# Six tiles' gates worked out in the last tile, gate matrices by ScalarE, fewer routing steps

## What is computed

```python
def hier_moe(h, w_group, b_group, w_expert, b_expert, w_gate_up, w_down):
    gl = tok @ w_group + b_group
    p_group = softmax(gl);  p_top, g_idx = top_k(p_group, 1)
    el = (tok @ w_expert + b_expert).reshape(-1, N_GROUPS, EXPERTS_PER_GROUP)
    e_val, e_idx = top_k(take_along_axis(el, g_idx), TOP_K)
    e_w = softmax(e_val) * p_top                  # the two gates of a token
    for e in range(N_EXPERTS):                    # 16 experts, D_EXPERT = 256
        gu = tok @ w_gate_up[e]
        act = silu(gu[:, :256]) * gu[:, 256:]
        y = y + gates[:, e:e + 1] * (act @ w_down[e])
```

## Time and profile before

| | us |
|---|---|
| median of 3 runs | 980.98 (979.95 to 981.66) |
| profiled execution | 977.75 |
| its span | 975.9 |
| PE busy | 927.5 (95%) |
| DVE busy | 593.3 (61%) |
| ACT, POOL busy | 234.6 (24%), 217.0 (22%) |
| mean granted TensorE clock | 0.995 |

### The profile page before, as it was taken

The page is one execution under the profiler, slowest core; times in us unless marked ns, Lnnn a source line. Parts: engine busy times, 40 slices in busy tenths (PEclk is TensorE's granted clock), DMA queues, the critical chain, the costliest instruction groups (busy, mean ns, idle before and its releaser), DMA issues.

```text
span 975.9 us, 19077 instructions
## 1 busy us (share of the span) xinstructions
PE 927.5 (95%) x7577; PEld 681.8 (70%) x7577; DVE 593.3 (61%) x1812; ACT 234.6 (24%) x606; POOL 217.0 (22%) x302
## 2 busy tenths in 40 slices
PE   5999999999999999999999998889999999999995
PEld 5787687596686868769769676565667666777663
DVE  2366775784685687487578468988534324345443
ACT  1233331431431342234143233231010111111010
POOL 7020020020011002002002000400244454465653
PEclk9999999999999999999999999999999999999998
DMA  8920101020010110110100002812557976979621
GB/s 305 395 91 1 45 22 45 1 66 22 23 66 1 45 45 22 44 36 32 44 2 23 21 24 71 339 67 66 179 171 238 343 232 215 346 260 357 219 91 57
DMA packets 51491, 113.99 MB, mean 117 GB/s; under 512 B 11191, under 2 KB 14519, under 8 KB 51392
## 3 DMA queue, kind: packets, MB, share of 16 engines
q1 hardware_dynamic: 35072, 87.07, 24.9%
q0 software_dynamic: 14592, 25.22, 7.7%
q10 hardware_dynamic: 1728, 0.31, 0.2%
HBM read 112.54 MB, written 25.17 MB: 141 GB/s over the span
## 4 chain that ended last, share of the span: by engine, by line
PE 78%; DVE 16%; DMA 2%; issue 2%; ACT 1%; SPq 0%; POOL 0%; POOLq 0%; DVEq 0%; ACTq 0%
PE pm L417 71%; PE pm L420 6%; DVE pqkv L1405 4%; DMA w_sb<-in_w_in 2%; DVE X L1558 1%; DVE bs L1623 1%; DVE sc L1628 1%; DVE xT L1344 1%; DVE hT L1360 1%; PE pm L798 1%; DMA qkvT<-h_mid,w_sb 0%; DVE V_S L1636 0%; DVE xT L1223 0%; ACT pqkv L978 0%; DVE y_mix L1649 0%
## 5 line engine op out<-in xcount | busy, mean ns | idle before, releaser
L417 PEld LDWEIGHTS pm<-hT,w_sb 128*128 128x128 f32 x1544 | 177.0, 194 | 9.5 <-DVE hT L1360 6.0
L417 PE MATMUL pm<-hT,w_sb 128*128 128x128 f32 x1544 | 178.9, 278 | 4.9 <-DVE hT L1360 4.3
L417 PE MATMUL pm<-w_sb,hT 128*128 128x512 f32 (+1 forms) x384 | 148.1, 534 | 0.4 <-DMA w_sb<-in_w_in 0.4
L1918 POOL TENSOR_TENSOR tail<-tail,rows 128x512 f32<-128x512 f32 x8 | 10.2, 1269 | 511.4 <-ACT aTm L999 511.4
L417 PE MATMUL pm<-wo_sb,pT 128*128 128x512 f32 x256 | 115.0, 596 | 2.8 <-ACT pT L1046 2.1
L417 PEld LDWEIGHTS pm<-w_sb,hT 128*128 128x128 f32 x384 | 70.7, 191 | 57.1 <-issue 52.9
L417 PE MATMUL pm<-ctmp,w_sb 128*128 128x128 f32 x768 | 88.8, 276 | 1.1 <-DVE ctmp L1706 1.1
L1405 DVE SCALAR_TENSOR_TENSOR pqkv<-ci,cw,pqkv 128x128 f32<-128x128 f32 x288 | 77.6, 344 | 19.9 <-ACT pqkv L978 19.6
L417 PEld LDWEIGHTS pm<-ctmp,w_sb 128*128 128x128 f32 x768 | 86.7, 192 | 2.6 <-issue 2.0
L417 PEld LDWEIGHTS pm<-wo_sb,pT 128*128 128x128 f32 x256 | 46.7, 190 | 53.0 <-issue 49.3
L1778 DVE TENSOR_TENSOR ci<-pm,gain 128x512 f32<-128x512 f32 x32 | 20.6, 686 | 82.6 <-PE pm L798 48.7
(11 more groups left out here) (315 smaller groups left out, 1527.0 us busy)
## 6 DMA issues: line engine op xcount, KB each, us to landing
w_sb<-in_w_gate_up SPq DMA_DIRECT2D x12, 2048.0 KB, 14.8
w_sb<-in_w_down SPq DMA_DIRECT2D x12, 1024.0 KB, 6.5
w_sb<-in_w_in SPq DMA_DIRECT2D x4, 2048.0 KB, 20.5
wo_sb<-in_w_gate_up SPq DMA_DIRECT2D x4, 2048.0 KB, 14.6
xt<-in_x SPq DMA_DIRECT2D x8, 512.0 KB, 4.4
xT<-in_x_turned SPq DMA_DIRECT2D x8, 512.0 KB, 3.5
wo_sb<-in_w_out SPq DMA_DIRECT2D x1, 4096.0 KB, 21.8
sc<-in_x SPq DMA_DIRECT2D x8, 512.0 KB, 3.5
```

What stands on the lines that cost most here:

```text
L417: return pe.matmul(o_, lhsT=l_, rhs=r_, start=start, stop=stop, skip_group_check=True)
L1918: g.tensor_tensor(qk_in[:, 0:QH, :], qk_in[:, 0:QH, :], gqk[:, None, 0:DH].broadcast_to([P, QH, DH]), ALU.mult)
```

## The change

It has four parts.

1. `rsqrt_one` replaces `rsqrt` for the two factors of one column each (the norm of x in `row_factors`, the norm before the experts in `factor`): ten steps in place of twelve, 16 times in the program.
2. `route_experts` and `route_rows` do both choices in one instruction of twice the width: 2 steps in place of 4, and 6 in place of 10.
3. The gates of the first six tiles are worked out in `late(7)` between `add_x(0)` and `add_x(1)` (five steps). They are divided by the token's number (`gate_by_row`; one more step makes the reciprocals `by_row`), and ScalarE makes `hot_gate[u]` as `hot_row[u]` times that factor. TensorE sums 12 of the 16 gate products between the counts and the half slots, where `keep_busy` products stood; the last four come behind `turn_halves(0)`, and the two halving products behind `gate_up_halves(0)`. `hot_mod` 0 to 7 lie in a new place (`more`), since `ci` is written earlier than they are last read.
4. In the routing of the last two tiles each pair of `row_hots` signals by itself (`R.hots`), the sum that needs the new picks comes last, and `rows_of` reads pm[0] directly, with the copy to `table` behind it.

```diff
+EARLY_HOTS = [c * NT + t for c in range(TOPK) for t in range(AHEAD)]
+LATE_HOTS = [c * NT + t for c in range(TOPK) for t in range(AHEAD, NT)]
...
             keep_busy(pm[3], 3)
+            pe.wait_ge(A.rank_ready, 1)
+            mm(pm[1][:, 0:n], ones[:, :], before, True, False)
             pe.wait_ge(R.picks, 1)
-            pe.wait_ge(A.rank_ready, 1)
-            mm(pm[1][:, 0:n], upper_strict, picks[:, AHEAD * NE:], True, False)
...
-            mm(pm[1][:, 0:n], ones[:, :], before, False, True).then_inc(R.counts, 1)
+            mm(pm[1][:, 0:n], upper_strict, picks[:, AHEAD * NE:], False, True).then_inc(R.counts, 1)
...
-            keep_busy(pm[3], 4)
-            pe.wait_ge(R.hots, 1)
-            for u in late_hots:
-                ins = mm(pm[0][:, 0:P], hot_mod[u], hot_row[u], False, u == late_hots[-1])
+            def add_gates(first, last):
+                for i, u in enumerate((EARLY_HOTS + LATE_HOTS)[first:last]):
+                    pe.wait_ge(R.gate_hots, first + i + 1)
+                    ins = mm(pm[5][:, 0:P], hot_mod[u], hot_gate[u], first + i == 0, u == LATE_HOTS[-1])
+                return ins
+
+            add_gates(0, 8)
+            for i, u in enumerate(LATE_HOTS):
+                pe.wait_ge(R.hots, i + 1)
+                ins = mm(pm[0][:, 0:P], hot_mod[u], hot_row[u], False, u == LATE_HOTS[-1])
             ins.then_inc(R.rows_summed, 1)
-            keep_busy(pm[3], 1)
-            pe.wait_ge(R.rows_ready, 1)
+            add_gates(8, len(EARLY_HOTS))
+            pe.wait_ge(R.rows_ready, 2)
...
-            keep_busy(pm[3], 2)
+            keep_busy(pm[3], 1)
             turn_rows(0)
...
+                if i < NE:
+                    turn_halves(i)
                 if i == 0:
                     sum_gates()
-                if i < NE:
-                    turn_halves(i)
...
                 gate_up_halves(i)
+                if i == 0:
+                    sum_half_gates()
...
+            def gate_hot(u):
+                act.activation(hot_gate[u], hot_row[u], ACT.Copy,
+                               scale=gate_by_row[:, u // NT, u % NT:u % NT + 1]).then_inc(R.gate_hots, 1)
+            act.wait_ge(A.hots, TOPK * AHEAD + 1)
+            for u in EARLY_HOTS:
+                gate_hot(u)
             act.wait_ge(R.exp_in, 1)
...
+            act.wait_ge(R.hots, len(LATE_HOTS) + 1)
+            for u in LATE_HOTS:
+                gate_hot(u)
...
+            def rsqrt_one(step, y, a, tmp, src, scale):
+                step(v.tensor_scalar(a, src, scale, EPS, ALU.mult, ALU.add))
+                step(v.tensor_scalar(y.bitcast(I32), a.bitcast(I32), 1, None, ALU.logical_shift_right))
+                step(v.tensor_scalar(y.bitcast(I32), y.bitcast(I32), -1, RSQRT_MAGIC, ALU.mult, ALU.add))
+                for c in (1, -2):
+                    step(v.scalar_tensor_tensor(tmp, y, a, y, ALU.mult, ALU.mult))
+                    step(v.scalar_tensor_tensor(y, tmp, -3.0 * c * c, y, ALU.add, ALU.mult))
...
+                tt(prod_of[:, :, ts], picks_of[:, :, ts], ranks.unsqueeze(1).broadcast_to([P, TOPK, n, NE]), ALU.mult)
+                route_step(v.tensor_reduce(rank_of[:, :, ts], prod_of[:, :, ts], AX_X, ALU.add))
...
             def late(t):
                 f = Late(t)
                 v.wait_ge(R.iotas, 2)
+                route_step(v.reciprocal(by_row.rearrange("p c t -> p (c t)"), row_f.rearrange("p c t -> p (c t)")))
                 rows_ahead()
                 f.add_x(0)
+                v.wait_ge(A.exp_out, 1)
+                gates(0, AHEAD).then_inc(A.hots, 1)
                 f.add_x(1)
...
-                    ins = row_hots(c, t)
-            ins.then_inc(R.hots, 1)
+                    row_hots(c, t).then_inc(R.hots, 1)
             v.wait_ge(R.rows_summed, 1)
-            step(v.tensor_copy(table[:, 0, :], pm[0][:, 0:P]))
-            rows_of(table[:, 0, 0:NE], NE, slot_rows).then_inc(R.rows_ready, 1)
+            rows_of(pm[0][:, 0:NE], NE, slot_rows).then_inc(R.rows_ready, 1)
+            v.tensor_copy(table[:, 0, :], pm[0][:, 0:P]).then_inc(R.rows_ready, 1)
...
-            step(gates(0, NT))
-            for t in range(NT):
-                gate_hot(0, t).then_inc(R.gate_hots, 1)
+            gates(AHEAD, NT - AHEAD).then_inc(R.hots, 1)
             copy_rows(0)
-            for t in range(NT):
-                gate_hot(1, t).then_inc(R.gate_hots, 1)
```

More of the change, by code:

```diff
@@ L155, in build @@
         ring = [(part(KD, 2 * DE), part(DE // P, D)) for _ in range(RING - 1)]
-        left = part(D)
+        left, more = part(D), part(D)
         og, es, e1, e2, scratch = [part(NT, GROUPS, early=True) for _ in range(5)]
@@ L163, in build @@
         rank = part(AHEAD, NE)
[L164 removed]
+        rank_of, expert_of, mod_of, comb_of, gate_of, by_row, gate_by_row = [part(TOPK, NT) for _ in range(7)]
         past_ranks = part(TOPK, NT, RANKS)
```

58 lines of the change are left out of this document (25 added, 33 removed).

## The result

Five executions of the changed kernel have a median of 971.14 us (970.95 to 973.1). Beside them on the same chip the kernel before has 980.02 us (978.22 to 981.66). The ratio is 0.9915, 95% interval 0.9897 to 0.9932; by it the change saves 8.3 us, and the two medians lie 8.9 us apart. The prediction said 974.5 us, with a range from 972.6 to 977.4. Its sum for the profiled execution was 977.75 - 6.5 = 971.2, and the profiled execution of the changed kernel takes 971.03. So the sum came out, and the step from the one execution to the median did not.

The account below looks back on a forecast made before the run. TensorE was taken to bound the kernel, with savings only where it waits on the chain around start, tile 7, routing and first expert. 0.2 + 2.8 - 0.5 + 4.0 = 6.5 us, median 980.98 to 974.5, range 972.6 to 977.4.

Parts of the forecast that it names:

- The sum: All terms along the path together: 0.2 + 2.8 - 0.5 + 4.0 = 6.5 us saved, profiled execution 977.75 to 971.2.
- two fewer save 0.39: Factors with ten steps for twelve, 0.193 us a step: 0.39 saved in tile 7 and in `late(7)`, 0.98 in all.
- At the start: Tile 1's first factor: 0.2 us saved, not 0.39, as the copy to hT can't start before 54.31.
- Tile bodies: Factors in the tiles between: nothing saved, since VectorE waits for TensorE there; a rival gave 971 to 973, chance 0.07.
- Part 3 in `late(7)`: Gate steps on VectorE before the second `add_x`: net +0.04 us against 0.99 us of cover, so nothing.
- ScalarE's twelve matrices: The `gate_hot` matrices after ScalarE's last scaling: 0.30 us each, lying between 677 and 681 us.
- The steps up to the slots: Routing of the last tiles, from counts to slots: 0.23 + 0.79 + 0.69 + 0.32 = 2.03 us saved.
- The gather: First gather: starts 2.8 us earlier, overlaps the fourth expert's weight load and lands 0.5 us later for it.
- Behind the first `gate_up`: From first `gate_up` to the halves' products: 8.92 for 13.41 us, less halving products 0.45, net 4.0 saved.
- The step that failed: From profiled execution to median: the median of the runs lies 3.2 us above, so 980.98 to 974.5.
- The clock rival: TensorE loses its full clock in the wait before the first turn: 3.0 us more, 977.5; chance 0.09.

Follow-up runs that it names:

- e3: The kernel before with only the ten-step factors in place of twelve-step ones: 979.2 us, 0.9999 of the kernel before.
- e1: The kernel before, unchanged, run against itself: 979.58 us, ratio 0.9997.
- e11: The changed kernel with the load of the fourth expert's weights held back until the first gather has landed: 970.96 us.
- e2: The changed kernel, unchanged, run again on the same chip as the kernel before: 971.9 us, 0.992 of the kernel before.
- e5: The changed kernel with the last four gate products, table copy and halving products back between first gate_up and the half's turn: 974.0 us, 0.9928 of the kernel before.
- e4: The changed kernel with the twelve-step factors put back: 973.57 us, 0.9943 of the kernel before.
- e12: The kernel before with two unread products, at its waits of 0.39 and 0.80 us by the first expert's halves; another chip: 1007.77 us, 0.9994.
- e15: Second run of the kernel before with two unread products at its waits of 0.39 and 0.80 us; another chip: 1011.11 us, 1.0009.

## Why the prediction came out as it did

**The sum** came out within 0.2 us: 971.2 for the profiled execution, 971.03 measured. Part of that is luck, as two errors of 0.4 us cancel. It also took both profiled executions to have one stretch at 1.2 GHz each, ahead of the one at the end that all have. The terms one by one:
- Part 1, "two fewer save 0.39": mis-sized. A factor saves 0.20, since "the new steps are of the same kinds and size" fails for three of them (0.25 apart). So part 1 is 0.6 us, not 0.98. At the start the saving is 0.21 as forecast, but not because the copy to `hT` can't start before 54.31: in e3 the product that it needs is over 0.6 us before it starts, and the distance is shorter by the same 0.2; it is simply all that a factor saves. The other 0.39 of the 0.60 in the table is luck: the second block of tile 0 waits for the load of `w_in` and begins at 21.22 instead of 21.61, and anywhere from 21.2 to 22.3 us over the traces of e1 to e11. Tile bodies: nothing, as said.
- Part 3 in `late(7)`, nothing: right. VectorE waits 0.92 us before the second `add_x` where it waited 0.99.
- ScalarE's twelve matrices lie at 676.7 to 680.3, as said.
- The steps up to the slots: 1.97 measured for 2.03, each of the four within 0.03.
- The gather, "I take 0.5 off": 0.31 longer in this trace, but not for the reason given; in e11, without the load beside it, it is as long.
- Behind the first `gate_up`: 3.92 for 4.0. TensorE waits 1.43 us for the gather, as said (1 to 2.5).

**The step that failed** is "the median of the runs shown, 3.2 us above that, from 980.98 to 974.5". It carried the distance between one execution and a median over as if it belonged to the kernel. That distance is made of stretches at 1.2 GHz: the profiled execution of before had one and was among its fastest, most of its executions have two or three, the changed kernel's one or two, as their mean clocks tell. The medians lie 8.9 us apart (980.02 and 971.14) and 7.6 in e2; 6.7 of it, 6.0 to 7.0 by single clocks, are the change at equal clock, and the rest goes with fewer such stretches. The 3.2 itself was too large, as it rested on three executions: the median of 46 executions of before is 979.6, 1.8 us above its profiled one. And for the changed kernel the distance is 0.11 us in the first five executions (971.14 and 971.03), while e2's profiled execution is the slowest of its five. Nothing tied the 3.2 to the changed kernel; 977.75 - 6.5 was the better forecast of the lower end, and the median should have been put 0 to 3 us above it.

**The clock rival** was priced with one execution as its witness against: "the wait of 1.53 us at 55.85 left those 128 passes at full rate". In e1 the clock did fall there, behind 2.19 us, and in e5 behind 1.98, but not in e4 behind 2.20. None of the three traces with a wait of 1.5 us there shows it, but e2 does at the first turn, behind 1.29. A single trace can't rule out what happens in a part of the executions. Its price was too high as well: 0.9 us (e2) to 1.7 us (e1), where 3.0 was taken from nine idle us.

**Still open**: why the changed kernel's executions hold fewer such stretches. The change takes one of the places away (e1's at 712 us), which would fit, but e12 and e15 do not show it, on chips with a larger scatter of their own, and on those chips the changed kernel's mean clock is no higher. Ten executions without one at 0.991, where 15 of 46 had it before, would come by chance about once in 50 times ((31/46)^10 = 0.02), with the mark at 0.991 chosen after the fact. Chance is not ruled out.
